# Nine rows of expert fetches at the start of the context stage, the others spread evenly behind them

## What is computed

```python
sc = jnp.einsum('thsk,hsnk->thsn', qp, subkeys)
top_s, top_i = lax.top_k(sc, PEER_TOPK)
...
best_s, best_p = lax.top_k(cand_s, PEER_TOPK)
expert = jnp.take_along_axis(cand_i, best_p, axis=-1)
g = jax.nn.softmax(best_s, axis=-1)
act = jax.nn.gelu(jnp.einsum('thkd,td->thk', u_tab[expert], xt))
return jnp.einsum('thk,thkd->td', g * act, v_tab[expert])
```

## Time and profile before

| | us |
|---|---|
| median of 3 runs | 4549.07 |
| lowest, highest | 4547.99, 4556.22 |
| the profiled execution | 4545.71 |
| its span on the core | 4544.0 |
| mean granted clock of TensorE | 0.867 |

### The profile page before, as it was taken

The page is one execution under the profiler, slowest core; times in us unless marked ns, Lnnn a source line. Parts: engine busy times, 40 slices in busy tenths (PEclk is TensorE's granted clock), DMA queues, the critical chain, the costliest instruction groups (busy, mean ns, idle before and its releaser), DMA issues. The chain is left out here.

```text
span 4544.0 us, 44585 instructions
## 1 busy us (share of the span) xinstructions
PE 3758.4 (83%) x12065; PEld 1571.2 (35%) x12065; DVE 2790.3 (61%) x6341; ACT 1641.4 (36%) x5133; POOL 1635.5 (36%) x1312
## 2 busy tenths in 40 slices
PE   8999999999999689999776888898777566676666
PEld 6654455656554233443221223342222111111110
DVE  1122777577676976645898557445678984544444
ACT  4211445232213343334344334333344553333333
POOL 0000223223222333333444444443444445555453
PEclk9999999999999799999887899999887666666666
DMA  8645688789999989999999999999999999999998
GB/s 345 233 163 214 261 335 330 276 303 377 372 407 405 365 352 401 378 381 407 411 398 337 420 414 397 395 403 412 407 398 382 393 397 414 414 421 414 414 421 348
DMA packets 277595, 1671.68 MB, mean 368 GB/s; under 512 B 30496, under 2 KB 47968, under 8 KB 90848
## 3 DMA queue, kind: packets, MB, share of 16 engines
q0 software_dynamic: 184320, 1342.26, 73.7%
q1 hardware_dynamic: 84864, 303.14, 17.4%
q10 hardware_dynamic: 8160, 23.43, 1.6%
HBM read 1630.93 MB, written 37.78 MB: 367 GB/s over the span
## 5 line engine op out<-in xcount | busy, mean ns | idle before, releaser
L1103 POOL DMA_INDIRECT slots<-in_peer,idxR x1280 | 1629.2, 1273 | 2834.1 <-PE ps L1416 1775.6
L1416 PE MATMUL ps<-slots,lhs 128*64 128x512 f32 x4544 | 1489.6, 770 | 686.9 <-ACT lhs L1158 668.9
L1705 DVE CUSTOM_DVE_ANT_0 slots<-slots,h2R 128x1024 f32<-128x1024 f32 x1280 | 1546.1, 1224 | 737.0 <-issue 676.1
L1398 PE MATMUL ps<-ring,arena 128*128 128x512 f32 (+1 forms) x3264 | 1379.9, 579 | 13.3 <-ACT arena L1348 6.8
L1416 PEld LDWEIGHTS ps<-slots,lhs 128*64 128x64 f32 x4544 | 294.9, 158 | 1773.9 <-ACT lhs L1158 1521.3
L1398 PEld LDWEIGHTS ps<-ring,arena 128*128 128x128 f32 x3264 | 628.7, 197 | 780.3 <-issue 764.7
L1147 ACT ACTIVATE gelus<-dots 128x1 f32<-128x1 f32 x1280 | 256.6, 200 | 1487.9 <-DVE dots L1705 1458.2
L1158 ACT ACTIVATE lhs<-fold,wgts 128x64 f32<-128x64 f32 x1136 | 395.4, 348 | 37.1
L1150 ACT ACTIVATE wgts<-gelus,gsmR 128x1 f32<-128x1 f32 x1280 | 377.4, 295 | 42.5 <-ACT gelus L1147 0.5
L1398 PE MATMUL ps<-ring,slots 128*128 128x512 f32 (+1 forms) x576 | 221.6, 545 | 0.0
L1717 DVE SCALAR_TENSOR_TENSOR slots<-slots,wgts 128x1024 f32<-128x1024 f32 x135 | 173.1, 1282 | 79.0 <-ACT wgts L1150 73.3
(11 more groups left out here) (206 smaller groups left out, 2416.0 us busy)
## 6 DMA issues: line engine op xcount, KB each, us to landing
ring<-in_whead SPq DMA_DIRECT2D x48, 1024.0 KB
ring<-in_wa SPq DMA_DIRECT2D x48, 1024.0 KB
ring<-in_wq SPq DMA_DIRECT2D x32, 1024.0 KB
slots<-in_peer,idxR POOLq DMA_INDIRECT x1280
ring<-in_wgc SPq DMA_DIRECT2D x16, 1024.0 KB
ring<-in_wgb SPq DMA_DIRECT2D x16, 1024.0 KB
ring<-in_wout SPq DMA_DIRECT2D x16, 1024.0 KB
o_scratch<-inb SPq DMA_DIRECT2D x80, 128.0 KB
```

Source lines behind the costliest of these rows:

```text
L1103: g.indirect_dma_start(out=slot(R), out_offset=None, in_=a["peer"], in_offset=bass.IndirectOffsetOnAxis(ap=idxR[:, p % KEEP, g2, col:col + ...
L1398: done = mm(out, lhsT, rhs, start=n == 0, stop=n == KD - 1)
L1416: done = mm(ps[j * HALF:(j + 1) * HALF, g2, :], weights, slot(R)[:, D + j * UW:D + (j + 1) * UW], start=start, stop=stop)
L1705: v.tensor_tensor_reduce(out=u, in0=u, in1=h2R[:, g2, :], scale=1.0, scalar=0.0, op0=ALU.mult, op1=ALU.add, accum_out=dots[:, R % LHS:R % ...
```

## The change

The linear share of rows in the first stage is given a start: at the first event of the stage the planner asks for `FEW + PE_LAG` = 9 rows at once, and spreads the other 247 over the stage. The later stages are as before.

```diff
@@ -523,10 +523,10 @@
             weight = spare if k == len(GROUPS) - 1 else wall
             total = sum(weight[a:b])
             rows = min(len(cs) * ROWS, total / ROW_TIME if k == len(GROUPS) - 1 else len(cs) * ROWS)
-            spent = 0.0
+            spent, ahead = 0.0, FEW + PE_LAG if k == 0 else 0
             for n in range(a, b):
                 spent += weight[n]
-                due[n + 1] = BASE[k] * ROWS + rows * spent / total
+                due[n + 1] = BASE[k] * ROWS + ahead + (rows - ahead) * spent / total
         self.loaded, self.tail, self.x_at, self.gt_at, row = set(), [], 0, 0, 0
         placed, first, last = [], None, None
         for n, ev in enumerate(self.front):
```

## The result

| | us |
|---|---|
| before, median of 5 runs | 4549.56 |
| after, median of 5 runs | 4568.99 (4562.70 to 4571.07) |
| ratio, with its 95% interval | 1.0038 (1.0027 to 1.0048) |
| the profiled execution of after: span | 4567.3 |

What follows compares the result with a forecast made beforehand. PE's order of work was taken to set the pace for most of the context stage, with gathers joining late and DVE last. Start loss 14 (10.3 + 3 + 1) less late gain 4 gave +10: 4559 against the median, range 4541 to 4571.

Steps and rivals of the forecast that it cites:

- the forecast case: Whole kernel: start loss 14, late gain 4, so +10 and 4559 against the median; own range 4554 to 4565; chance 0.45.
- worse: Through event 177, DVE and queues delay PE, clock falls twice: loss 22 to 26, gain 3, about 4570; chance 0.11.
- the late gain: Mainly from 1138 to 1590 us: fewer gathers left, so PE waits less; gain of 4 us, bounds 0 and 11.
- Where the rows go, and that nothing else changes: Context stage: 9 rows more at event 163, 6.4 at 252; rows 80 to 223 chained as before, PE and DVE sums unchanged.
- PE's wait for row 0: Start of the context stage: PE stands from 502.17 to 516.4, 14.2 us instead of 1.89.
- Rows 0 to 5, and the last scores: Start: rows follow at DVE's pace of 1.15 to about 522.5; event 164 is done at 523.6 instead of 505.19.
- The first `hq`: Behind event 164: PE does rows 6 and 7 as their fetches land, and `hq` starts at about 530.
- The clock, 3: Rows 0 to 5 at the start: two to four run at half clock after the gap; 2 to 4 us more.
- The transfers: From dot 8, rows wait for DMA queues, DVE may be late; PE's rows 12 to 16 held 0 to 6, 1 taken.
- The early rows come back in full: The 9.3 us of early rows return, rows 0 to 79 being PE's before event 254 in both kernels; net zero.
- repaid: Whole stage: start loss 8 to 10, late gain 8 to 11, ending at 4548 to 4552, no change; chance 0.27.
- Faster: Late part: gathers are the true bound; fewer rows behind event 252 give 17, loss 7, about 4538; chance 0.14.

Runs made afterwards that it cites:

- warm2: The changed kernel with 14 extra matmuls on PE in its wait for row 0, into a bank that holds nothing yet; 1.0030 against the kernel before.
- p164: The changed kernel with all nine rows ahead placed behind event 164 instead of 163; 1.0014 against the kernel before.
- s6: The changed kernel with six rows ahead instead of nine, placed behind event 168 (the first `hq`) instead of 163; 1.0044 against the kernel before.
- p168: The changed kernel with all nine rows ahead placed behind event 168 (the first `hq`) instead of 163; 1.0012 against the kernel before.
- experiments 3 to 5: Changed kernel with extra matmuls in PE's wait (14: 1.0030); with six rows ahead behind event 168 (1.0044); with nine spread over later events (0.9997 to 1.0008).

## Why the prediction was right, and where its sizes were off

The direction and the mechanism of the start held, and the time lies in the wide range of 4541 to 4571. But it lies near its upper end, above the 4554 to 4565 of the forecast case itself and nearer to "worse" (4570), and the late gain came out right by luck. By its steps:

- **Where the rows go, and that nothing else changes.** Held: the engines' sums are within 2 us, and the chained runs are the same.
- **PE's wait for row 0.** Forecast 14.2, measured 14.20. DVE's end of `topc` and the delay from dot to matmul set it.
- **Rows 0 to 5, and the last scores.** Forecast 522.5 and 523.6. Measured 524.6 and 525.6 (525.54 and 526.63, less 0.99). The six rows took 8.18, with a granted clock of 0.50 from 517 to 521 us; I had put that into a later term.
- **The first `hq`.** Forecast 530, measured 534.3. Row 7's dot ended at 529.9 (530.93 less 0.99), 1.4 to 2.4 late, its matmuls took 1.97, and then `hT` was still not there (1.34).
- **The clock, 3.** By warm2 it was worth 4.4 at the end of the first `hq` and 0.4 at event 180. As a term of a sum it was wrong to add it: it stands beside the transfers.
- **The transfers.** This is the term that was mis-sized. I let `hT` wait behind gathers only until the first `hq`, and gave DVE and the queues together 1 us behind it. The loads took 16.7 us to land instead of 5.9, held up the second projection as well (2.89), and put the first part of it at the half clock (0.50 from 550.4 to 553; 8.77 instead of 7.13). Event 177 came at 570.7 instead of 562.6, or 566.6 with the 3 and the 1, and the start lost 19.2 instead of 14 (bounds 7 and 22; 18.3 with the prediction's 1.03 for a row). The waits for `hT` and what the second projection lost by them are 5.9 of it (1.34 + 2.89 + 1.64), and p164, which has none of them, lost 6.5 less.
- **The early rows come back in full.** Held: between events 180 and 255 the loss without them stays at 19.2 to 19.6. Only the place was off: at event 255 PE of the kernel before still has five of rows 0 to 79 to do.
- **The late gain, 4.** The size held in the profile (19.2 at event 180, 14.9 at 2135 us), by luck, for the place and the reason did not. All of it came in the scans of head 2, where a wait of 3.59 and the low clock with it became 1.2, and before 1138 us, where I had written that the shift would stay within 3. Behind that, fewer gathers gave nothing in sum. The wait of 5.09 at 1271 us did shrink to 0.36, and others grew (the next one for a chain from 4.14 to 5.05, one for ACT from 3.4 to 4.7). That the gain is there in exactly the orders without the wait of 3.6, and that s6, with two rows less ahead behind event 252, loses 10 late where this one loses nothing, speaks for a gain of order and not of transfer time.

The rivals: "repaid" did not come, for the loss was twice what it asked; p168 and p164 are closer to it. "Faster" would have needed a late gain of 16, and no order tried had one. "Worse" (4570, a loss of 22 to 26 at the start and a gain of 3) lies 1 us from the measured median, the forecast (4559) 10. Its reason, the queues holding PE up through event 177, is what the forecast had too low; but its loss at the start did not come (19.2), and the second fall of the clock came behind the wait for `hT` and was no cause of its own.

## What to carry to other kernels

Where all engines follow one list in order, look first for the engine that makes the others wait: here it was DVE, and rows put ahead of the matmul engine's other work only made that engine wait for DVE. The rows of a bunch whose data lay in the slots were nearly free; those beyond ran at the pace of one fetch after the other, and everything behind them on the matmul engine, another queue's loads included, was late with them. Before adding up a clock loss and a transfer, ask whether they run beside each other. And where the change shifts the whole later order by a few rows, try it with the start undone and with the later part undone: here the start was worth 19 us, and in s6, whose order behind event 252 differs from that of before by four rows at most, the later part 10.

## What was not expected of the hardware

- Keeping the matmul engine busy through a wait raised its granted clock behind it (1.00 instead of 0.50; six rows in 5.53 us instead of 8.18) and left 0.4 us of gain at event 180, for the loads that came next landed after 16.9 us as against 16.7.
- Five loads of 512 KB took a median of 5.9 us to land where no gathers moved (before, p164) and 16.7 beside the gathers of six slots (after).
- One 128x512 float32 matmul stands in the profile as two MATMULs of 0.43 us each at the full clock: 28 of them took 24.20 us and 14 took 12.18.
- Two profiled executions of one kernel differ by 4 us within this stage, with the same waits in the same places; 15 runs of the kernel before, made beside experiments 3 to 5, ranged from 4543.84 to 4560.08 us.
